# Sixteen modulation tiles as direct fp32 products with the weights stationary, in a two-layer diffusion step on one core

## The reference

```python
mod = jax.nn.silu(cond) @ w_ada[layer] + b_ada[layer]      # (1024) @ (1024, 6144)
shift1, scale1, gate1, shift2, scale2, gate2 = jnp.split(mod[:, None, :], N_MOD, axis=-1)
h = rmsnorm(x, norm_mix_g[layer]) * (1 + scale1) + shift1
# even layer: mixer_ab, one projection h @ w_in_ab, DeltaNet and a short conv, one projection out
# odd layer: multiscale_pool
x = x + gate1 * y
h = rmsnorm(x, norm_ffn_g[layer]) * (1 + scale2) + shift2
x = x + gate2 * conv_ffn(h, ...)
```

## Time and profile before

| | |
|---|---|
| median of three runs | 1753.28 us |
| profiled execution | 1756.97 us, span 1755.2 us |
| TensorE busy | 1592.5 us, 91% of the span |
| VectorE busy | 961.7 us |
| GpSimd busy | 790.0 us |
| ScalarE busy | 432.2 us |
| HBM read | 146.19 MB, mean 85 GB/s |

### The profile page before, as it was taken

One profiled execution on the slowest core, in us unless ns is written; L12 is line 12 of the kernel. 1 busy time (PEld: TensorE's weight loads), 2 busy tenths in 40 slices (PEclk: granted clock), 3 DMA queues, 4 the chain that ended last, 5 costly groups with the idle time before them and its releaser, 6 DMA issues.

```text
span 1755.2 us, 28178 instructions
## 1 busy us (share of the span) xinstructions
PE 1592.5 (91%) x10867; PEld 1536.4 (88%) x10867; DVE 961.7 (55%) x1320; ACT 432.2 (25%) x692; POOL 790.0 (45%) x492
## 2 busy tenths in 40 slices
PE   3799997888898879799999999998799999999996
PEld 2599995777887769699999999997699999999996
DVE  4654123566655365587878788873543315524554
ACT  4542213222332351511001101114533201100112
POOL 0244441556546413355565465552045445544543
PEclk9899998899999989899999999999899999999998
DMA  8121220111111112134443253320012222222222
GB/s 327 37 72 60 72 72 24 60 50 60 58 64 49 37 37 75 69 123 162 157 138 122 103 180 135 120 96 34 24 60 72 75 81 72 69 75 84 72 69 75
DMA packets 42490, 150.12 MB, mean 86 GB/s; under 512 B 4544, under 2 KB 5696, under 8 KB 41920
## 3 DMA queue, kind: packets, MB, share of 16 engines
q1 hardware_dynamic: 42432, 149.35, 25.0%
HBM read 146.19 MB, written 3.15 MB: 85 GB/s over the span
## 4 chain that ended last, share of the span: by engine, by line
PE 83%; DVE 8%; ACT 4%; issue 3%; DMA 1%; POOL 0%; ACTq 0%; DVEq 0%; SPq 0%; POOLq 0%
PE ps L591 65%; PE ps L766 3%; PE ps L749 3%; PE ps L606 3%; PE ps L764 3%; DVE attn L1437 1%; PE ps L865 1%; ACT work L934 1%; PE ps L817 1%; DMA x<-in_x 1%; PE ps L728 1%; PE ps L618 1%; DVE work L1415 1%; PE ps L819 1%; PE ps L680 0%
## 5 line engine op out<-in xcount | busy, mean ns | idle before, releaser
L504 POOL TENSOR_SCALAR whi<-raw 128x1024 fp32r<-128x1024 f32 (+1 forms) x172 | 184.6, 1073 | 751.8 <-PE ps L591 602.1
L591 PE MATMUL ps<-hhi,whi 128*128 128x320 f32 x1984 | 459.5, 313 | 31.9 <-DVE hlo L1271 31.7
L591 PE MATMUL ps<-hlo,whi 128*128 128x320 f32 x1984 | 454.9, 311 | 0.0
L591 PE MATMUL ps<-hhi,wlo 128*128 128x320 f32 x1984 | 454.7, 311 | 0.0
L507 POOL TENSOR_TENSOR wlo<-raw,whi 128x1024 fp32r<-128x1024 f32 (+1 forms) x172 | 429.7, 2498 | 14.3
L591 PEld LDWEIGHTS ps<-hhi,whi 128*128 128x128 f32 x1984 | 334.8, 190 | 38.2 <-issue 26.0
L591 PEld LDWEIGHTS ps<-hlo,whi 128*128 128x128 f32 x1984 | 334.9, 190 | 0.0
L591 PEld LDWEIGHTS ps<-hhi,wlo 128*128 128x128 f32 x1984 | 334.7, 190 | 0.0
L591 PE MATMUL ps<-hidhi,whi 128*128 128x320 f32 x704 | 161.3, 310 | 4.7 <-POOL wlo L507 3.3
L591 PE MATMUL ps<-hidlo,whi 128*128 128x320 f32 x704 | 161.0, 310 | 0.0
L591 PE MATMUL ps<-hidhi,wlo 128*128 128x320 f32 x704 | 160.9, 310 | 0.0
(11 more groups left out here) (181 smaller groups left out, 1902.3 us busy)
## 6 DMA issues: line engine op xcount, KB each, us to landing
raw<-in_w_gu SPq DMA_DIRECT2D x88, 512.0 KB, 3.3
ada_raw<-in_w_rows SPq DMA_DIRECT2D x48, 512.0 KB, 3.6
raw<-in_w_in SPq DMA_DIRECT2D x28, 512.0 KB, 3.2
raw<-in_w_dn SPq DMA_DIRECT2D x32, 448.0 KB, 3.3
ada_first<-in_w_ada SPq DMA_DIRECT2D x4, 2048.0 KB, 22.7
ada_raw<-in_w_ada SPq DMA_DIRECT2D x16, 512.0 KB, 3.2
raw<-in_w_ada SPq DMA_DIRECT2D x16, 512.0 KB, 3.3
raw<-in_w_dn SPq DMA_DIRECT2D x16, 512.0 KB, 3.4
```

Of the source, the lines that this page charges most:

```text
L504: nc.gpsimd.tensor_scalar(whi[s][:, 0:n], raw[s][:, 0:n], 1.0, 0.0, ALU.mult, ALU.add).then_inc(s_whi, 1)
L591: last = nc.tensor.matmul(pair[pr][:, b], wt[s][:, cs], act[:, k, b * HALF:(b + 1) * HALF], start=(j == 0 and q == 0), stop=(j == len(tile ...
```

## The change

The sixteen first tiles are laid out in memory like the other weights (128 output columns per tile, all 1024 inputs, as `w_first`). Each tile is multiplied as it lies, in fp32: a block of 128x128 weights is stationary, and the two columns of silu(c), silu(c_ctx) move. Eight matmuls accumulate into the two PSUM columns where `add_batch(0)` reads. Hi and lo parts, row copies and `ada_columns` of these tiles go. The tiles come in six DMAs of 4, 4, 4, 2, 1 and 1 tiles. POOL no longer waits for the sixteen tiles. SP raises the five semaphores by what the removed steps would have counted. `c_parts` stays for tiles 16 to 47.

```diff
-        more = [nc.alloc_sbuf_tensor_at(f"more{j}", [P, SLOT], F32R, ...) for j in range(4)]
+ADA_CHUNKS = [4, 4, 4, 2, 1, 1]
...
             for sm in (*s_ev.values(), s_conv, s_silu, s_aff, s_h, s_hid_hi, s_l2ln):
                 sp.sem_inc(sm, PRIMED)
+            for sm in (s_ada_hi, s_ada_lo):
+                sp.sem_inc(sm, ADA_FIRST)
+            for sm in (s_ada_cp, s_ada_t):
+                sp.sem_inc(sm, ADA_FIRST // 2)
...
-            n = ADA_FIRST // 4
-            for q in range(4):
-                sp.dma_start(ada_first[:, n * q:n * (q + 1), :],
-                             t["w_ada"][n * q:n * (q + 1)].rearrange("u p f -> p u f")).then_inc(s_ada1[q], 16)
+            at = 0
+            for q, n in enumerate(ADA_CHUNKS):
+                sp.dma_start(ada_first[:, at:at + n, :],
+                             t["w_first"][at:at + n].rearrange("u p f -> p u f")).then_inc(s_ada1[q], 16)
+                at += n
...
-            pool.wait_ge(s_ada_pe, ADA_FIRST)
             for s in range(2):
                 split(s, 0, s, guard=False)
...
             norm_sums(0)
-            pe.wait_ge(s_c_parts, 1)
-            for g in range(ADA_FIRST // 2):
-                ada(2 * g)
-                if g:
-                    ada_columns(g - 1)
-                ada(2 * g + 1)
-            ada_columns(ADA_FIRST // 2 - 1)
+            pe.wait_ge(s_silu_c, 1)
+            n = 0
+            for q, count in enumerate(ADA_CHUNKS):
+                pe.wait_ge(s_ada1[q], 16)
+                for _ in range(count):
+                    at = ADA_COLS + 2 * n
+                    for k in range(KD):
+                        last = nc.tensor.matmul(ps[:, col_bank[0], at:at + 2], ada_first[:, n, k * P:(k + 1) * P],
+                                                silu_c[:, k, :], start=(k == 0), stop=(k == KD - 1))
+                    last.then_inc(s_ada_pe, 1)
+                    n += 1
...
             def ada_hi(n):
-                if n < ADA_FIRST:
-                    if n % 4 == 0:
-                        act.wait_ge(s_ada1[n // 4], 16)
+                act.wait_ge(s_ada[n % 4], 16 * ((n - ADA_FIRST) // 4 + 1))
+                if n >= ADA_FIRST + 2:
+                    act.wait_ge(s_ada_pe, n - 1)
                 else:
-                    act.wait_ge(s_ada[n % 4], 16 * ((n - ADA_FIRST) // 4 + 1))
...
             squares(0, (s_x0, s_x0), ((0, 2), (1, 2)))
-            for n in range(4):
-                ada_hi(n)
-                if n == 1:
-                    rsqrt_of_sums(0)
-            for g in range(ADA_FIRST // 2):
-                ada_copy(g)
-                for n in (2 * g + 4, 2 * g + 5):
-                    if n < ADA_FIRST:
-                        ada_hi(n)
+            rsqrt_of_sums(0)
             act.wait_ge(s_fold, 1)
             modulate(0, 0, 0)
...
-                dve.wait_ge(s_ada_t, batch_end[b] + 1)
+                if b:
+                    dve.wait_ge(s_ada_t, batch_end[b] + 1)
+                else:
+                    dve.wait_ge(s_ada_pe, ADA_FIRST)
...
-            for n in range(ADA_FIRST):
-                dve.wait_ge(s_ada_hi, n + 1)
-                hi, lo = ada_split(n)
-                nc.vector.tensor_tensor(lo[:], ada_source(n), hi[:].bitcast(F32),
-                                        ALU.subtract).then_inc(s_ada_lo, 1)
             add_batch(0)
```

More of the change, by code:

```diff
@@ L204, in build @@
         pe_tab = nc.alloc_sbuf_tensor_at("pe_tab", [P, 4, ROWS + GRID_W], F32, offset=off_h)
-        more = [nc.alloc_sbuf_tensor_at(f"more{j}", [P, SLOT], F32R, offset=off_h + 2048 + j * SLOT * 4)
-                for j in range(4)]
         assert ADA_FIRST * SLOT * 4 <= o4 - off_m
@@ L256, in build @@
         s_pe = sem("pe_loaded")
-        s_ada1 = [sem(f"ada_first_loaded{q}") for q in range(4)]
+        s_ada1 = [sem(f"ada_first_loaded{q}") for q in range(len(ADA_CHUNKS))]
         s_state = sem("state_loaded")
@@ L383, in ada_split @@
         def ada_split(n):
-            j = n % 4 if n < ADA_FIRST else n % 2
-            return (whi + more[0:2])[j], (wlo + more[2:4])[j]
+            return whi[n % 2], wlo[n % 2]
         def ada_source(n):
-            return ada_first[:, n, :] if n < ADA_FIRST else (ada_raw + raw)[n % 4][:]
+            return (ada_raw + raw)[n % 4][:]
         block = ctx.enter_context(nc.Block())
@@ L401, in load_ada @@
                 sp.wait_ge(s_ada_lo, n + (ADA_FIRST - 3))
-                sp.dma_start((ada_raw + raw)[s][:], t["w_ada"][n + ADA_FIRST]).then_inc(s_ada[s], 16)
+                sp.dma_start((ada_raw + raw)[s][:], t["w_ada"][n]).then_inc(s_ada[s], 16)
             def load_rows(n):
@@ L421, in _ @@
             for s in range(2):
-                sp.dma_start(ada_raw[s][:], t["w_ada"][ADA_FIRST + s]).then_inc(s_ada[s], 16)
+                sp.dma_start(ada_raw[s][:], t["w_ada"][s]).then_inc(s_ada[s], 16)
             sp.dma_start(lmask[:], t["lmask"]).then_inc(s_lmask, 16)
@@ L428, in _ @@
             for s in range(2):
-                sp.dma_start(raw[s][:], t["w_ada"][ADA_FIRST + 2 + s]).then_inc(s_ada[2 + s], 16)
+                sp.dma_start(raw[s][:], t["w_ada"][2 + s]).then_inc(s_ada[2 + s], 16)
             with sp.Fori(1, (ADA_LAST - ADA_FIRST) // 4) as i:
@@ L959, in ada_hi @@
             def ada_hi(n):
-                if n < ADA_FIRST:
-                    if n % 4 == 0:
-                        act.wait_ge(s_ada1[n // 4], 16)
-                else:
-                    act.wait_ge(s_ada[n % 4], 16 * ((n - ADA_FIRST) // 4 + 1))
-                back = 4 if n < ADA_FIRST else 2
-                if n >= back:
-                    act.wait_ge(s_ada_pe, n - back + 1)
+                act.wait_ge(s_ada[n % 4], 16 * ((n - ADA_FIRST) // 4 + 1))
+                if n >= ADA_FIRST + 2:
+                    act.wait_ge(s_ada_pe, n - 1)
+                else:
+                    act.wait_ge(s_unit, 28)
                 nc.scalar.activation(ada_split(n)[0][:], ada_source(n), ACT.Copy).then_inc(s_ada_hi, 1)
@@ L1654 @@
     w_ada = np.concatenate([a["w_ada"][0], a["w_ada"][1]], axis=1)
-    groups = w_ada[:, :ADA_LAST * P].reshape(2, 4, P, ADA_LAST // 2, ADA_COLS)
-    arrays["w_ada"] = np.ascontiguousarray(groups.transpose(3, 0, 2, 1, 4).reshape(ADA_LAST, P, SLOT))
+    arrays["w_first"] = tiles(w_ada[:, :ADA_FIRST * P], KD)
+    groups = w_ada[:, ADA_FIRST * P:ADA_LAST * P].reshape(2, 4, P, (ADA_LAST - ADA_FIRST) // 2, ADA_COLS)
+    arrays["w_ada"] = np.ascontiguousarray(groups.transpose(3, 0, 2, 1, 4).reshape(ADA_LAST - ADA_FIRST, P, SLOT))
     arrays["w_rows"] = np.ascontiguousarray(w_ada[:, ADA_LAST * P:].T.reshape(ADA_ROWS, P, D))
```

## The result

The changed kernel takes 1773.05 us in the median of four runs (1767.69 to 1776.67), against 1753.32 us (1751.21 to 1753.43) before: a ratio of 1.0113, 95% interval 1.0085 to 1.0141. It is 19.7 us slower; the forecast was 17.6 slower, at 1771 us. The profiled execution took 1771.61 us with a span of 1769.8, 14.64 us above the profiled execution of before.

The account below looks back on a forecast made before the run. The prediction took TensorE (83% of the span) as the bound, through the start of the L591 stream: tiles +21.0 and POOL's splits -3.4 make +17.6 us, from 1753.28 to about 1771 us, range 1766 to 1778.

Parts of the forecast that it names:

- What bounds it: TensorE is 83% of the span; the first 80 us count only through when the L591 product stream starts.
- Price of a pair: In the sixteen first tiles: each of 256 weight-load-and-matmul pairs costs 0.11 us at 2.4 GHz, 0.213 at 1.2 GHz.
- Which clock: In the sixteen first tiles: full clock for 3.5 us, then 1.2 GHz; bias at 80.9 instead of 59.90, +21.0 us.
- POOL's splits: Between bias and stream: POOL splits the first two units earlier, not beside DVE's norm; -3.4 us, between -3.8 and -2.
- Loads and parts: At the start: loads don't set the pace, six parts gain nothing; added semaphore increments counted 0, range 0 to 0.6 us.
- The sum: Whole kernel: 21.0 - 3.4 = +17.6 us, giving 1771 us on the median, 1.0% slower.
- The first rival: In the sixteen first tiles: the full clock holds; with POOL's gain -5.5 us, 1747.8 us, faster; chance 0.13.

Follow-up runs that it names:

- `poolwait`: The changed kernel with only POOL's wait for the sixteen first tiles put back: 1779.82 us, ratio 1.0163 to the kernel before.

## Why the prediction was right

- **What bounds it.** The start of the stream decides, as said; from it to the gate sums it is 209.4 us in both kernels. SP adds four increments, not the five of the text on the change; four are in its diff and in the prediction.
- **Price of a pair.** 0.11 and 0.213 us were taken from L618, L689 and L728. The changed kernel gives the same, and the run with 128 columns 28.60/256 = 0.112. That products add up in the same two columns costs nothing that shows. The price in the Trainium skill (TensorE: Matmul & The Clock Gate, section "LDWEIGHTS (loading the stationary operand)"), 107 ns for 128 columns with no second price for a throttled array, agrees at full clock and doesn't hold at half clock (0.213).
- **Which clock.** Half, from 33.2 to the end, 3.5 us after the first product (3.5 predicted). This was the step on which the sign hung, and the run with 128 columns confirms its reason: what moves, not how long TensorE is busy (with the limits named under that run). That the 3.5 us came out is partly luck: they were taken from two falls of the clock after other work (the second lies at 63.3 by its window, not 63.35), and with equal code up to there the clock fell 2.8 us after the first product in the run with four parts and 2.7 in `poolwait`. The bias came at 81.27 against 80.9; the 0.4 us is the start of the products, 29.7 and not 29.35.
- **POOL's splits.** -3.4 predicted, -3.4 between the two traces. Undone by itself the term is 4.2 to 4.3, since POOL then starts later against the bias than it did in the kernel before.
- **Loads and parts.** Nothing, as said, by the run with four parts. The added increments delay SP's first issue by 0.23 us (1.53 against 1.30) and don't show behind it: the square sums start at 25.32 against 25.66.
- **The sum.** +17.6 predicted and +18.0 measured at the stream's start; +14.6 in the profiled executions, +19.7 in the medians. The 3.4 us between the first two lie in code that is the same. The other 5.1 are scatter: the profiled execution lies 3.7 above the median in the kernel before and 1.4 below it in the changed one. The changed kernel's four runs spread over 9 us, so that the median came within 2 us of the forecast is partly luck; the start of the stream is what bears the sum out.
- **The first rival** (full clock, 1747.8 us) was not what the change did, but its number is near what the change gives once its condition is met: 1748.86 and 1750.19.

## What to carry to other kernels

Before replacing wide products by a few narrow ones, ask at which clock they will run: a long stretch of weight loads with 2 moving columns ran at 1.2 GHz and cost twice its price at full clock, and streaming the same two columns 64 times over took 23 us off it. A released buffer can be worth more than the arithmetic that was saved: here all that the kernel with 128 moving columns gained at first came from POOL's splits leaving DVE's way, and the rest from starting the tiles ahead of the square sums. Small parts of a load were worth nothing where the consumer didn't wait for the load. Whether they help once it starts earlier was not run: the early order was tried with six parts only.

## What was not expected of the hardware

The granted clock reads 1.00 before the first change that the trace holds, whatever the engine does. In the kernel with 2 moving columns and the early order this row covers ten microseconds of pairs:

```profile
30.00:40.00 10.00, 10.00 (x49) 10.00 (x49) 0.00 (x0) 0.00 (x0) 3.01 (x2) 1.00 0.92 367
```

27.44 us for 128 pairs is 0.214 a pair, which elsewhere goes with a clock of 0.50. The first change that this trace holds is the fall at 56.1. The same shows in the kernel with 128 columns and the early order, where 13 rows stand in the first window, from 17.29 on, and 44 in the second:

```profile
17.00:20.00 3.00, 2.71 (x13) 2.74 (x14) 2.90 (x5) 1.42 (x3) 0.00 (x0) 1.00 1.01 412
20.00:25.00 5.00, 5.00 (x44) 5.00 (x44) 2.41 (x5) 2.85 (x4) 0.00 (x0) 1.00 1.02 412
```

At the start of a trace the spacing of equal rows tells the clock, and the column doesn't. Read so, the two traces say more on the change's own question. Started at half clock, the pairs with 2 moving columns stayed there for 27 us and ran faster only after the square sums, whose products move 320 columns; the pairs with 128 moving columns, started at half clock too, ran at 0.11 from about 20.5 on, with no other products ahead of them.
